# Two transformer blocks on one core: last stage partly on TensorE with a 0/1 matrix, and two stages' first weights divided ahead

## What is computed

```python
# block 1: windowed attention with sink (16 heads of 64, 4 groups), then
y = attention @ att_w_o ; x = x + g1 * rmsnorm(y) ; swiglu ...
# block 2: mLSTM branch y_m and latent attention branch y_a (8 heads of 128)
merged = g_m * (y_m @ w_branch_m) + g_a * (y_a @ w_branch_a)
x = x + gate1 * (merged @ w_out)
# mixture of experts: 32 experts, top 2, slots in blocks of 128
out = lax.map(run_block, ...)                       # per block: (silu(x Wg) * (x Wu)) Wd * weight
y = zeros((T, D)).at[slot_tok].add(out.reshape(cap, D))
x = x + gate2 * y
return rms_norm(x, final_norm_g)
```

## Time and profile before

| what | us |
|---|---|
| runs | 3177.13, 3182.32, 3200.04; median 3182.32 |
| the profiled execution, its own time | 3180.01 |
| its span | 3178.0 |
| mean granted clock of TensorE over the span | 0.972 of full speed |
| TensorE busy | 2963.4 |
| last product ends | 3129.5 |
| last VectorE operation ends | 3174.0 |

### The profile page before, as it was taken

One profiled execution on the slowest core, in us unless ns is written; L12 is line 12 of the kernel. 1 busy time (PEld: TensorE's weight loads), 2 busy tenths in 40 slices (PEclk: granted clock), 3 DMA queues, 4 the chain that ended last, 5 costly groups with the idle time before them and its releaser, 6 DMA issues. The chain is left out here.

```text
span 3178.0 us, 39383 instructions
## 1 busy us (share of the span) xinstructions
PE 2963.4 (93%) x14311; PEld 2367.6 (74%) x14311; DVE 1669.7 (53%) x2591; ACT 1256.9 (40%) x1906; POOL 778.7 (25%) x387
## 2 busy tenths in 40 slices
PE   7999988999989999899999899999999997999993
PEld 4777775887778878677777788778868775888882
DVE  6444477522654326835444212443452326999996
ACT  4444434222232223334333321222131216899994
POOL 1111010444434434210000122121112221444440
PEclk9999998999999999999999999999999998999997
DMA  6100053222543235310000122101211224778773
GB/s 234 34 20 7 1 205 139 93 97 84 213 143 119 99 113 217 120 47 21 13 13 0 60 73 81 44 36 53 86 53 67 91 84 173 253 269 274 257 260 130
DMA packets 87734, 347.63 MB, mean 109 GB/s; under 512 B 21332, under 2 KB 27764, under 8 KB 76608
## 3 DMA queue, kind: packets, MB, share of 16 engines
q1 hardware_dynamic: 62568, 310.80, 26.9%
q0 software_dynamic: 17856, 16.85, 2.4%
q10 hardware_dynamic: 7192, 18.48, 1.6%
HBM read 377.94 MB, written 47.79 MB: 134 GB/s over the span
## 5 line engine op out<-in xcount | busy, mean ns | idle before, releaser
L3309 DVE TENSOR_TENSOR ex_g_lo<-ex_g_raw,ex_g_hi 128x1024 fp32r<-128x1024 f32 x188 | 221.0, 1218 | 2.0 <-ACT ex_g_hi L3248 2.0
L3248 ACT CAST ex_g_hi<-ex_g_raw 128x1024 fp32r<-128x1024 f32 x188 | 191.8, 1052 | 3.0 <-PE psum L3194 3.0
L1144 DVE TENSOR_TENSOR ff_gated<-psum,ff_silu 128x512 f32<-128x512 f32 x44 | 30.4, 692 | 307.4 <-PE psum L582 307.4
L526 POOL TENSOR_TENSOR ff0i_w_lo<-ff0i_w_raw,ff0i_w_hi 128x1024 fp32r<-128x1024 f32 x43 | 109.5, 2547 | 175.8 <-ACT ff0i_w_hi L486 135.9
L3192 PE MATMUL psum<-ex_g_hi,ex_x_hi 128*128 128x512 f32 x376 | 151.6, 403 | 0.0
L3193 PE MATMUL psum<-ex_g_lo,ex_x_hi 128*128 128x512 f32 x376 | 147.6, 393 | 0.0
L3194 PE MATMUL psum<-ex_g_hi,ex_x_lo 128*128 128x512 f32 x376 | 147.5, 392 | 0.0
L3155 POOL DMA_INDIRECT expert_sums<-ex_o,token_ids x47 | 90.0, 1915 | 230.6 <-DMA expert_sums<-ex_o,token_ids 147.3
L526 POOL TENSOR_TENSOR ff1i_w_lo<-ff1i_w_raw,ff1i_w_hi 128x1024 fp32r<-128x1024 f32 x43 | 110.6, 2572 | 142.7 <-ACT ff1i_w_hi L486 142.7
L582 PE MATMUL psum<-ff_h_hi,ff0i_w_hi 128*128 128x512 f32 x352 | 138.3, 393 | 6.5 <-ACT ff_h_hi L757 6.5
L582 PE MATMUL psum<-ff_h_hi,ff1i_w_hi 128*128 128x512 f32 x352 | 138.1, 392 | 5.0 <-POOLq L523 5.0
(11 more groups left out here) (572 smaller groups left out, 8125.3 us busy)
## 6 DMA issues: line engine op xcount, KB each, us to landing
ex_g_raw<-in_w_experts_gu_dram SPq DMA_DIRECT2D x32, 2048.0 KB, 9.0
ex_d_raw<-in_w_experts_d_dram SPq DMA_DIRECT2D x32, 1024.0 KB, 9.7
ff0i_w_raw<-in_ffn_in_dram SPq DMA_DIRECT2D x44, 512.0 KB, 3.2
ff1i_w_raw<-in_ffn_in_dram SPq DMA_DIRECT2D x44, 512.0 KB, 3.2
wom_w<-in_mod_w_dram SPq DMA_DIRECT2D x8, 2048.0 KB, 8.0
ff0o_w_raw<-in_ffn_out_dram SPq DMA_DIRECT2D x15, 704.0 KB, 5.2
ff1o_w_raw<-in_ffn_out_dram SPq DMA_DIRECT2D x15, 704.0 KB, 6.4
ga_w_raw<-in_w_merge_a_dram SPq DMA_DIRECT2D x16, 512.0 KB, 3.2
```

The source lines that it names most:

```text
L526: nc.gpsimd.tensor_tensor(w_lo[:, v % 2, :], w_raw[:, v % 2, :], w_hi[:, v % 2, :].bitcast(F32), ALU.subtract).then_inc(lo_made, 1)
L1144: nc.vector.tensor_tensor(gated[:], sums, silu[:], ALU.mult).then_inc(gated_made, 1)
L3248: nc.scalar.copy(cols(g_hi, n), cols(raw.g_raw[i % 3], n)).then_inc(q["g_hi_made"], 1)
L3309: nc.vector.tensor_tensor(cols(g_lo, n), cols(raw.g_raw[i % 3], n), cols(g_hi, n).bitcast(F32), ALU.subtract).then_inc(q["g_lo_made"], 1)
```

## The change

Three parts. (1) `Combine`: the last block's product is no longer stored and added in DRAM. VectorE multiplies it by the gate out of PSUM, it is divided, and TensorE multiplies it with a 0/1 matrix (slot to token) and adds it in PSUM to the gated sums of the earlier blocks; for tiles 0 to 3 TensorE adds the residual too (product with the identity), for tiles 4 to 7 POOL adds it to the gated sums. Square and final multiplication read PSUM. The sums are loaded once all stores but the last have landed, in the order 4, 0, 1, 5, 2, 6, 3, 7. (2) The first weights of "wo" are loaded, rounded and subtracted within the last group of the band attention. (3) Those of "ga" likewise in the last head of the latent attention. In (2) and (3), ACT rounds four halves, then the second weights, then the other four halves (`between=4`).

The diff, cut to its core:

```diff
@@ -109,6 +109,10 @@
+
+    def end_pool(self, pool):
+        pool.wait_ge(self.hi_made, 1)
+        self.chip.nc.gpsimd.tensor_tensor(self.lo[:, 0, :], self.raw, self.hi[:, 0, :].bitcast(F32), ALU.subtract)
...
@@ -421,6 +425,7 @@
+    second_early = halves is not None and halves.between is not None
...
@@ -491,19 +496,25 @@
                 if not ready:
                     split(0, 0, 16)
                 if halves:
-                    halves.on_act(act)
+                    halves.on_act(act, (lambda: split(1, 1, 16)) if second_early else None)
             if "act" in start:
                 start["act"](act)
             def body(j, is_last, steps):
                 for v in range(steps):
-                    if not (is_last and v == steps - 1) and not (two_early and isinstance(j, int) and j == 0 and v == 0):
+                    if not (is_last and v == steps - 1) and not ((two_early or second_early) and isinstance(j, int) and j == 0 and v == 0):
                         split((v + 1) % 2, per * j + v + 1, 16 * (chunks * j + (v + 1) // 2 + 1))
                     if on_act and v % chunks == chunks - 1:
                         u = v // chunks
                         on_act(act, j, u, sums(u), used, chunks * (2 * j + u + 1) + 2)
-            pairs(act, body, unroll)
+            if second_early and not unroll:
+                body(0, False, per)
+                with act.Fori(1, n_pairs - 1) as j:
+                    body(j, False, per)
+                body(n_pairs - 1, True, tail)
+            else:
+                pairs(act, body, unroll)
...
@@ -1500,6 +1513,8 @@
+            sp.wait_ge(projected, 3 * AG)
+            ahead.end_sp(sp)
...
@@ -1516,6 +1531,7 @@
             groups(pool, body)
+            ahead.end_pool(pool)
...
@@ -1532,6 +1548,8 @@
                 for p in range(NP + 3):
                     if more and p in (3, 5, 7):
                         split_hi(g + 1, (3, 5, 7).index(p))
+                    if not more and p == 9:
+                        ahead.end_act(act)
...
@@ -1677,8 +1696,13 @@
-    def on_act(self, act):
-        self.round(range(self.first, self.n_k))
+    def on_act(self, act, second=None):
+        if second:
+            self.round(range(self.first, self.between))
+            second()
+            self.round(range(self.between, self.n_k))
+        else:
+            self.round(range(self.first, self.n_k))
...
@@ -1886,6 +1910,8 @@
+            sp.wait_ge(projected, 3 * MH)
+            ahead.end_sp(sp)
...
@@ -1893,6 +1919,8 @@
+            pool.wait_ge(turned_q, 3 * MH)
+            ahead.end_pool(pool)
...
@@ -1924,6 +1952,8 @@
+                    if not more and u == 4:
+                        ahead.end_act(act)
...
@@ -3116,7 +3146,7 @@
-    psum_o = chip.psum[:, 5:7, :].rearrange("p h t -> p (h t)")
+    psum_o = chip.psum[:, 6:8, :].rearrange("p h t -> p (h t)")
...
@@ -3158,6 +3188,9 @@
+            if i == LAST - 1:
+                pool.wait_ge(q["x_turned"], LAST)
+                combine.count_tokens(nc.gpsimd)
...
@@ -3170,10 +3203,10 @@
-        store(LAST)
-        pool.wait_ge(stored[0], 16 * ((N_BLK + 1) // 2))
-        pool.wait_ge(stored[1], 16 * (N_BLK // 2))
+        pool.wait_ge(stored[0], 16 * ((LAST + 1) // 2))
+        pool.wait_ge(stored[1], 16 * (LAST // 2))
         pool.sem_inc(combine.ready, 1)
+        combine.on_pool(pool)
...
@@ -3213,7 +3246,7 @@
-                    mm = products(chip.psum[:, 5 + s, :], ((a_hi[:, u, n * P:(n + 1) * P], a_lo[:, u, n * P:(n + 1) * P]),
+                    mm = products(chip.psum[:, 6 + s, :], ((a_hi[:, u, n * P:(n + 1) * P], a_lo[:, u, n * P:(n + 1) * P]),
...
@@ -3226,7 +3259,7 @@
-            mm = nc.tensor.matmul(chip.psum[:, 7, 0:N_BLK], in_blk[:, i, :], of_blk_w[:, i, :],
+            mm = nc.tensor.matmul(chip.psum[:, 5, 0:N_BLK], in_blk[:, i, :], of_blk_w[:, i, :],
...
@@ -3237,7 +3270,9 @@
+        combine.start_pe(pe)
         down(LAST)
+        combine.on_pe(pe)
...
@@ -3291,6 +3326,8 @@
+            if not more:
+                combine.start_act(act)
...
@@ -3298,7 +3335,6 @@
-        copy_out(LAST)
         combine.on_act(act)
...
@@ -3349,6 +3385,8 @@
+            else:
+                combine.start_dve(dve)
             gated(i)
             if more:
                 split_g(i + 1, 2)
@@ -3356,7 +3394,8 @@
             split_d(i, 0)
         split_a(LAST)
         split_d(LAST, 1)
-        combine.on_dve(dve)
+        dve.wait_ge(q["d_used"], DC * N_BLK)
+        combine.on_dve(dve, psum_o)
...
@@ -3364,75 +3403,172 @@
 class Combine:
+    PAIRS = (2, 0, 4, 6)
+    PAIR_OF = (0, 1, 2, 3, 0, 1, 2, 0)
+    ORDER = (0, 1, 2, 4, 5, 3, 6, 7)
+    ADDED = (4, 5, 6, 7)
+
+    def __init__(self, chip, x_tm, gate_r, token_ids, sums_dram, final_dram, out_dram):
...
+        last = expert_order()[N_BLK - 1]
+        self.last_ids = token_ids[:, last:last + 1]
+        self.e = [chip.place(f"co_e{u}", [P, 4, D], F32, at) for u, at in enumerate((A_AT + 32 * KIB, B_AT))]
+        self.tokens = chip.place("co_tokens", [P, S], F32, A_AT + 56 * KIB)
+        self.hot = chip.place("co_hot", [P, S], F32R, B_AT + 16 * KIB)
...
         self.e_in = [chip.sem(f"co_e_in{i}") for i in range(NB)]
+
+    def tile(self, t):
+        return self.e[t // 4][:, t % 4, :]
+
+    def bank(self, t, s):
+        return self.chip.psum[:, self.PAIRS[self.PAIR_OF[t]] + s, :]
+
+    def pair(self, t):
+        b = self.PAIRS[self.PAIR_OF[t]]
+        return self.chip.psum[:, b:b + 2, :].rearrange("p h t -> p (h t)")
     def start_sp(self, sp):
         sp.dma_start(self.fin_r[:], self.final_dram.broadcast_to([P, D])).then_inc(self.fin_in, 16)
     def on_sp(self, sp):
         sp.wait_ge(self.ready, 1)
+        for i in (4, 0, 1, 5, 2, 6, 3, 7):
+            sp.dma_start(self.tile(i), self.sums_dram[i * P:(i + 1) * P, :]).then_inc(self.e_in[i], 16)
+        for n, i in enumerate(self.ORDER):
+            sp.wait_ge(self.made, n + 1)
+            sp.dma_start(self.out_dram[i * P:(i + 1) * P, :], self.y[:, i, :]).then_inc(self.out_done, 16)
+        sp.wait_ge(self.out_done, 16 * NB)
+
+    def count_tokens(self, pool):
+        pool.iota(self.tokens[:], pattern=[[1, S]], base=0, channel_multiplier=0,
+                  allow_small_or_imprecise_dtypes=True).then_inc(self.counted, 1)
+
+    def on_pool(self, pool):
+        for n, i in enumerate(self.ADDED):
+            pool.wait_ge(self.to_add, n + 1)
+            self.chip.nc.gpsimd.tensor_tensor(self.tile(i), self.tile(i), self.x_tm[:, i, :], ALU.add).then_inc(self.added, 1)
+
+    def residual(self, pe, i):
+        for s in range(2):
+            self.chip.nc.tensor.matmul(self.bank(i, s), self.chip.ident[:], self.x_tm[:, i, s * HALF:(s + 1) * HALF],
+                                       start=True, stop=False)
+
+    def last_block(self, pe, i, start):
+        hot = self.hot[:, i * P:(i + 1) * P]
+        for s in range(2):
+            part = slice(s * HALF, (s + 1) * HALF)
+            self.chip.nc.tensor.matmul(self.bank(i, s), hot, self.o_hi[:, part], start=start, stop=False)
+            self.chip.nc.tensor.matmul(self.bank(i, s), hot, self.o_lo[:, part], start=False, stop=False)
+
+    def earlier_blocks(self, pe, i):
+        for s in range(2):
+            mm = self.chip.nc.tensor.matmul(self.bank(i, s), self.chip.ident[:], self.tile(i)[:, s * HALF:(s + 1) * HALF],
+                                            start=False, stop=True)
+        mm.then_inc(self.mixed, 1)
+
+    def start_pe(self, pe):
+        self.residual(pe, 0)
+
+    def on_pe(self, pe):
+        self.residual(pe, 1)
+        self.residual(pe, 2)
+        pe.wait_ge(self.hot_made, 1)
+        pe.wait_ge(self.o_lo_made, 1)
+        for i in (0, 1, 2):
+            self.last_block(pe, i, False)
+        pe.wait_ge(self.o_made, 1)
+        self.residual(pe, 3)
+        self.last_block(pe, 3, False)
+        for i in (0, 1, 2):
+            pe.wait_ge(self.scaled, i + 1)
+            self.earlier_blocks(pe, i)
+        for n, i in enumerate((4, 5)):
+            pe.wait_ge(self.made, n + 1)
+            self.last_block(pe, i, True)
+            pe.wait_ge(self.added, n + 1)
+            self.earlier_blocks(pe, i)
+        pe.wait_ge(self.scaled, 4)
+        self.earlier_blocks(pe, 3)
+        for n, i in enumerate((6, 7)):
+            pe.wait_ge(self.made, n + 3)
+            self.last_block(pe, i, True)
+            pe.wait_ge(self.added, n + 3)
+            self.earlier_blocks(pe, i)
+
+    def start_act(self, act):
+        self.chip.nc.scalar.activation(self.warm[:], self.chip.ones[:, 0:1], ACT.Sqrt)
     def on_act(self, act):
         nc, st = self.chip.nc, self.st
+        act.wait_ge(self.o_made, 1)
+        nc.scalar.copy(self.o_hi[:], self.o[:]).then_inc(self.o_hi_made, 1)
+        for n, i in enumerate(self.ORDER):
+            act.wait_ge(self.mixed, n + 1)
+            if n >= 1:
+                act.wait_ge(self.root, n)
```

(51 more changed lines are left out.)

76 lines of the change are left out of this document (22 added, 54 removed).

## The result

| what | us |
|---|---|
| the changed kernel | median 3169.1 of 11 runs (3160.3 to 3183.8) |
| the kernel before, same comparison | median 3191.0 of 11 runs (3177.1 to 3200.0) |
| ratio | 0.994, 95% interval 0.9925 to 0.9956 |
| the profiled execution after, its own time and its span | 3164.30, 3162.3 |

The change brings 0.6% by the ratio, some 19 us, where 24.7 were predicted; the two medians alone differ by 21.9. Its profiled span is only 15.7 us shorter. For a fair account the span is cut at products of TensorE, and each piece compared. The table has the lengths of the pieces for the kernels before and after and for the four that have only some of the change's parts (they are described under the experiments); the last piece runs from the last expert product to the end of the span.

A forecast was written before the change was run, and what follows sets the result against it. TensorE, busy 93% of the span, was taken as the bound outside its gaps and the last stage. Savings of 15.2 + 9.5 + 0 = 24.7 us from 3180.0 gave 3155.3, rounded to 3156 us; range 3147 to 3167.

The forecast's parts named there:

- Last stage: From the last expert product to the span's end: earlier loads and the new combine end it 15.2 us earlier.
- 2 fp32 products at 0.43 ... 1.8 us at full clock, below VectorE's 2.84: Last stage: identity products at 0.43 us each, so TensorE needs 1.8 us per late tile, below VectorE's 2.84.
- Collisions: Last stage: GpSimd's residual additions hold up VectorE's scalings, counted as 1.5 us, with ends 0 and 6.6.
- First merge: After the latent attention: early weights and a full clock end the first tile 9.5 us earlier; ends 6.9 and 10.
- With a gap of 1.7 us the clock has no reason to fall: First merge's start: TensorE pauses only 1.7 us, so its clock stays full; half clock would cost 2.6 us.
- rival (a): Last stage: TensorE's clock falls and products double, last y 7 us later, 3163 us in all; chance 0.10.
- Output projection: After the band attention: 5 us won at the start is given back in the middle, 0 net; ends +3 and -3.
- TensorE one step behind: Output projection: TensorE follows ScalarE's and VectorE's halves by one step, first tile ending at 434.2 against 434.5.
- rival (e): 47-block expert loop: moved banks and edits lengthen each block, 3184 us at 0.6 us a block; chance 0.03.
- Rival (b): Last stage: the store before the last lands in 6.4 us instead of 3.2, giving 3158 us; chance 0.10.
- Rival (d): Better than 1%: projection gains 3, no collisions or wait, earlier landing, shorter end, giving 3148 us; chance 0.07.
- Rival (c): Early weights bring less: half clock at the merge's start costs 2.6 us, projection loses 3, giving 3161; chance 0.10.

The follow-up runs named there:

- ga_only: Only the early first weights of the first merge, on the kernel before; merge 179.0 us against 185.5, last stage 47.6.
- wo_only: Only the early first weights of the output projection, on the kernel before; projection 105.4 us against 103.5.
- ga_warm: Changed kernel plus eight idle TensorE products in the last head of the latent attention; merge takes 176.8 us.
- wo_pe: Changed kernel, but TensorE instead of ScalarE makes the two increments that let it into the projection's first two tiles; projection 107.0 us.
- tail_ga: The change without its output projection part; ratio 0.9929 to the kernel before, median 3164.5 against 3184.1 us.

## Why the prediction was wrong, point by point

The time of 3156 was 13 us too low, and 3169.1 lies 2 us above the range. Two things add up. The change is worth 19 us and not 24.7. And the level was off: I started from a profiled execution of 3180.0 and a median of three of 3182.3, while in the comparison the kernel before had 3191.0 (3184.1, 3182.8 and 3183.4 in the later ones). Less 19, from my base, is 3161, inside the range; less 24.7, from 3191.0, is 3166.3, also inside it, barely. A third thing is an omission: the range's upper end adds 8, 6.9 and 0, though I had given the projection a lower end of -3. With it the range ends at 3170.4, counted from 3182.3, and the measured time lies inside.

By the means, 5.8 us of the 24.7 are missing: 2.7 in the merge, 1.9 in the projection, 1.2 in the last stage.

- **Last stage, predicted -15.2, measured -14.7 by the two profiles (48.5 to 33.8), -14.0 by means.** Right in size, partly by luck, since errors cancel, and with the wrong bound. Loads at 0.6 us ahead of the last product's end, the chain of the last block's product until 3.6 (3.8), table load and iota hidden: right. The failed step is "2 fp32 products at 0.43 ... 1.8 us at full clock, below VectorE's 2.84": they are 0.86 each, a late tile costs 2.65, the first finish starts at 12.7 instead of 11.1, and the end is TensorE's: with half of the products for the gated sums gone (tail_half) the last y comes 2.0 us sooner, with GpSimd's additions gone (tail_no_add) 1.0. The earlier trace rows held it already: two records for one product of `la_k` and `la_q`. The Trainium skill, "FP8 and Floating Point Precision", section "TensorE Precision Notes", says that true fp32 takes four passes through the array. That agrees roughly with the 0.86 us, 3.8 times the 0.227 of an fp32r product; by it the term would have been 4 x 0.227 = 0.91, an estimate. Collisions: 1.5 predicted, 3.0 seen, 1.0 paid. I had GpSimd's additions start when VectorE leaves its run of scalings; the first started at 3133.26, among them. The end of the span came 3.05 after the last y instead of 4.0; in ga_only and wo_only, with the old last stage, it came after 3.1 too, so this 1 us is of the profile of before and not of the change.
- **First merge, predicted -9.5, measured -6.5 (means -6.8).** The start at 1.8 us: right. The failed step is "With a gap of 1.7 us the clock has no reason to fall"; the "no gap is over 2.2 us" against rival (a) is the same step, and the trace of before speaks against both (above). It fell in each profile without idle products, for 3.4 or 6.8 us; my lower end, 6.9, was the answer. ga_warm shows that the clock is what is missing, and returns 2.2 of it.
- **Output projection, predicted 0, measured +2.0 (means +1.9).** The wait of ScalarE was found (5.39 for some 6). The failed step is "TensorE one step behind": I let TensorE follow the halves and did not see that its permission for the first banks stands on ScalarE's queue behind that wait. It thus started 2.8 us later than before, where I had it start early. The step that I did price, the idle time in the middle, never came about in the change; wo_pe, where it does (4.40 and 1.36 us idle, then half clock), takes 107.0, 3.5 us longer than before, close to the loss of 3 that I gave as this part's lower end.
- **47-block loop, rival (e): refuted**, 9.29 us a block in both. **Rival (b): refuted**, the loads that wait for the store were issued 2.8 us after it. **Rival (d)**, better than 1%: refuted by the ratio's interval, 0.9925 at the lowest. **Rival (a)**: clock 1.00 throughout; it appears in tail_half with a gap of 2.29. **Rival (c)**, clock at the merge and a projection that loses 3, is what happened, 5 us of its price; it had a chance of 0.10 and should have been the main case.

## What to carry to other kernels

When work is put ahead of a wait in one engine's program, list everything behind that wait, bare semaphore increments too: here one that costs nothing was what TensorE started on, and the early first weights paid only once it stood elsewhere, and with it the second rounding or its load. Count the records of a product before a duration is taken for it: fp32 shows two. Differences of 0.2% between single profiles are to be read piece by piece, since one stage without any edit moved here by 14 us.

## What was not expected of the hardware

- The clock differs between executions of the same code: the band attention took 334 us with 10.2 us of half clock in before and 348 us with 44.4 in tail_ga, neither with an edit in it; the other twelve profiles have 334 to 341 us. The merge's opening after the same pause of 1.82 us ran at half for 3.4 us in three profiles and 6.8 in five.
- A VectorE operation with one input in PSUM runs beside GpSimd unhindered: 1.28 us at 3145.51 beside the addition of 3145.48, while the next two, with both inputs in SBUF, took 3.37 us instead of the 2.35 of such a pair at 3131.96. The prediction had left this open; it agrees with the Trainium skill, "SBUF — State Buffer", section "SBUF: two separate sides", which has VectorE and GpSimd contend only when the VectorE operation has two SBUF inputs or runs in a mode that uses both ports.
- GpSimd is slowed in turn: the same addition takes 2.38 us when it starts beside a finish (3145.48), and 3.28 when it starts while a scaling is under way (3133.26).
